# GpSimd adds a head's gates half a head later and makes no low parts in the retrieval

## The reference

```python
def peer(h, w_q, sub_keys, u_tab, v_tab):
    q = (h @ w_q).reshape(B, T, PEER_HEADS, 2, PEER_HALF)
    s = jnp.einsum('bthpd,hpnd->bthpn', q, sub_keys)
    v1, i1 = lax.top_k(s[..., 0, :], K)
    v2, i2 = lax.top_k(s[..., 1, :], K)
    cand = (v1[..., :, None] + v2[..., None, :]).reshape(B, T, PEER_HEADS, K * K)
    cidx = (i1[..., :, None] * PEER_NKEYS + i2[..., None, :]).reshape(B, T, PEER_HEADS, K * K)
    top_s, pos = lax.top_k(cand, K)
    eidx = jnp.take_along_axis(cidx, pos, axis=-1)
    gates = jax.nn.softmax(top_s, axis=-1)
    ...
        u = jnp.take(u_tab, ib, axis=0)
        act = jax.nn.gelu(jnp.einsum('btd,bted->bte', hb, u), approximate=False)
        vv = jnp.take(v_tab, ib, axis=0)
        return jnp.einsum('bte,bted->btd', gb * act, vv)
```

## Time and profile before

| | us |
|---|---|
| median of 3 runs | 1904.72 (1902.17 to 1913.51) |
| profiled execution | 1909.61 |
| its span, first to last instruction | 1906.1 |
| mean granted TensorE clock | 0.963 |
| busy: TensorE | 1756.6 (92%) |
| busy: VectorE | 1314.3 (69%) |
| busy: GpSimd | 866.5 (45%) |
| busy: ScalarE | 716.8 (38%) |

### The profile page before, as it was taken

One profiled execution on the slowest core, in us unless ns is written; L12 is line 12 of the kernel. 1 busy time (PEld: TensorE's weight loads), 2 busy tenths in 40 slices (PEclk: granted clock), 3 DMA queues, 4 the chain that ended last, 5 costly groups with the idle time before them and its releaser, 6 DMA issues. The chain is left out here.

```text
span 1906.1 us, 28988 instructions
## 1 busy us (share of the span) xinstructions
PE 1756.6 (92%) x11226; PEld 1551.3 (81%) x11226; DVE 1314.3 (69%) x2623; ACT 716.8 (38%) x1133; POOL 866.5 (45%) x529
## 2 busy tenths in 40 slices
PE   4999999999989988898798779987999999999998
PEld 2667888888779978897798779986998888888887
DVE  5983444542242566875687779975868888888887
ACT  4442233322253323332332337772333333333334
POOL 2333222244434366676567655533534444444440
PEclk9999899999989989998898889998999999999999
DMA  9663221023214476686687659997979999999994
GB/s 347 232 232 112 101 79 35 24 89 100 88 56 165 158 219 191 197 241 185 182 217 211 201 164 307 332 327 248 361 264 353 376 376 371 372 373 374 374 362 154
DMA packets 187602, 436.05 MB, mean 229 GB/s; under 512 B 34376, under 2 KB 95944, under 8 KB 187360
## 3 DMA queue, kind: packets, MB, share of 16 engines
q1 hardware_dynamic: 113824, 275.29, 41.2%
q0 software_dynamic: 55296, 134.31, 22.3%
q10 hardware_dynamic: 18368, 24.94, 3.6%
HBM read 385.11 MB, written 49.35 MB: 228 GB/s over the span
## 5 line engine op out<-in xcount | busy, mean ns | idle before, releaser
L223 POOL DMA_INDIRECT own_rows<-in_peer_v_dram,own_row x128 | 211.5, 1652 | 266.8 <-DVE y_own L2139 258.1
L2033 PE MATMUL banks<-v_hi,coef_lo 128*128 128x512 f32 x756 | 294.4, 389 | 0.0
L2033 PE MATMUL banks<-v_lo,coef_hi 128*128 128x512 f32 x756 | 294.4, 389 | 0.0
L2033 PE MATMUL banks<-v_hi,coef_hi 128*128 128x512 f32 x756 | 294.1, 389 | 0.1
L246 POOL DMA_INDIRECT gate_scratch<-gates,add_at x128 | 213.4, 1668 | 106.8 <-DVE top_half L1619 51.2
L223 POOL DMA_INDIRECT own_rows<-in_u_rows_dram,own_row x128 | 165.0, 1289 | 190.9 <-DVE own_rows L1777 86.5
L1460 PE MATMUL banks<-h_hi,wring_hi 128*128 128x384 f32 (+2 forms) x560 | 200.7, 358 | 54.6 <-POOL wring_lo L1558 54.2
L1460 PE MATMUL banks<-h_lo,wring_hi 128*128 128x384 f32 (+2 forms) x560 | 199.0, 355 | 0.0
L1460 PE MATMUL banks<-h_hi,wring_lo 128*128 128x384 f32 (+2 forms) x560 | 198.2, 354 | 0.0
L2076 ACT ACTIVATE coef_hi<-coef 128x384 fp32r<-128x384 f32 x128 | 67.1, 525 | 272.8 <-DVE coef L2163 272.8
L1510 ACT ACTIVATE wring_hi<-weight_ring 128x1024 fp32r<-128x1024 f32 x68 | 72.2, 1061 | 252.3 <-PE banks L1460 250.8
(11 more groups left out here) (394 smaller groups left out, 4092.7 us busy)
## 6 DMA issues: line engine op xcount, KB each, us to landing
weight_ring<-in_peer_v_dram SPq DMA_DIRECT2D x128, 512.0 KB, 6.3
weight_ring<-in_peer_u_dram SPq DMA_DIRECT2D x88, 512.0 KB, 4.2
ada<-in_w_ada_dram SPq DMA_DIRECT2D x48, 512.0 KB, 5.9
gate_tiles<-gate_scratch SPq DMA_DIRECT2D x32, 768.0 KB, 7.5
gelu_scratch<-gelu_early ACTq DMA_DIRECT2D x112, 192.0 KB, 4.0
gelu<-gelu_scratch SPq DMA_DIRECT2D x112, 192.0 KB, 6.7
weight_ring<-in_w_merge_dram SPq DMA_DIRECT2D x32, 512.0 KB, 3.4
gate_scratch<-gate_block SPq DMA_DIRECT2D x32, 512.0 KB, 8.0
```

The costliest lines, as they stand in the source:

```text
L223: pool.indirect_dma_start(own_rows[:, n % R], None, tables[n // NS], bass.IndirectOffsetOnAxis(ap=own_row[:, n % NS:n % NS + 1], axis=0)). ...
L2033: last = nc.tensor.matmul(y_bank(t, half)[:], w[:, j, t * P:(t + 1) * P], x[:, j, c], start=(first and n == 0), stop=False)
```

## The change

1. `by_pool` is true only for n < DVE_FROM = 9: VectorE makes the other 27 low parts that GpSimd made, at their places in `fill`.
2. GpSimd's adds move by half a head. At j = 0 to 7 of head h it makes the second eight adds of head h - 2, at j = 8 it waits for the gates of head h - 1, and at j = 8 to 15 it makes the first eight adds of that head. The retrieval has 104 adds instead of 112, the scatter stage 24 instead of 16.
3. DOT_HEADS has 80 row products in the retrieval instead of 64. So U_DONE is 112 instead of 96, the expert stage uses 144 own rows instead of 160, and OWN_GELU is tile 7 instead of 12.

```diff
-DOT_HEADS, DOT_ITER = (0,) + (9,) * 6 + (10,), 8
-POOL_LO = True
+DOT_HEADS, DOT_ITER = (0,) + (11,) * 4 + (12,) * 3, 8
...
-OWN_GELU = 12
+OWN_GELU = 7
...
     if p < EXP_TILES - N_EARLY:
-        return 2 if p == OWN_GELU - 2 else 3
+        return 1 if p == OWN_GELU - 2 else 3
     if i >= 30:
         return int(j < 3)
-    return 2 if p % 11 == 0 else 1
+    return int(p % 18 > 0)
...
         def by_pool(n):
 
-            return n < DVE_FROM or POOL_LO and (n < FIRST[1] + HR and n % 2 == 0 or n % 4 == 2)
+            return n < DVE_FROM
...
-                for n in (*range(HR - 1, DVE_FROM), *pieces_of(0)):
-                    if by_pool(n):
-                        rest(n)
+                for n in range(HR - 1, DVE_FROM):
+                    rest(n)
                 at = 0
+                half = NSC * TOPK // 2
                 for h in range(1, PH):
                     before = sum(DOT_HEADS[:h])
                     pool.wait_ge(*V.after("own_row", h - 1))
-                    todo = pieces_of(h)
                     for j in range(TOPK):
-                        for n in todo[j * len(todo) // TOPK:(j + 1) * len(todo) // TOPK]:
-                            if by_pool(n):
-                                rest(n)
                         while at < before + R + DOT_HEADS[h] * (j + 1) // TOPK:
                             fetch(pool, at)
                             at += 1
-                        if j == 0:
+                        if j == TOPK // 2:
                             pool.wait_ge(*VG.after("gate", h - 1))
-                        for n in range(j * NSC, (j + 1) * NSC):
-                            add_gates(pool, h - 1, n)
+                        for n in range(j * half // 8, (j + 1) * half // 8):
+                            if n < half and h > 1:
+                                add_gates(pool, h - 2, half + n)
+                            elif n >= half:
+                                add_gates(pool, h - 1, n - half)
...
-                for n in range(NSC * TOPK):
-                    g_["add_gates"](pool, PH - 1, n)
-                    for m in range(n * (U_DONE - DOTS) // (NSC * TOPK), (n + 1) * (U_DONE - DOTS) // (NSC * TOPK)):
-                        fetch(pool, DOTS + R + m)
+                adds = [(PH - 2, n) for n in range(NSC * TOPK // 2, NSC * TOPK)] + [(PH - 1, n) for n in range(NSC * TOPK)]
+                for m in range(U_DONE - DOTS):
+                    for h, n in adds[m * len(adds) // (U_DONE - DOTS):(m + 1) * len(adds) // (U_DONE - DOTS)]:
+                        g_["add_gates"](pool, h, n)
+                    fetch(pool, DOTS + R + m)
```

## The result

| | before | after |
|---|---|---|
| median of 4 runs | 1906.06 us (1902.17 to 1913.51) | 1849.23 us (1843.21 to 1852.47) |
| ratio after/before, 95% interval | | 0.9694 (0.9654 to 0.9733) |
| span of the profiled execution | 1906.1 us | 1846.5 us |
| mean granted clock | 0.963 | 0.978 |

The change saves 57 us. The forecast was 1840 us and its range 1822 to 1876.

What follows compares the result with a forecast made beforehand. TensorE bounds the expert stage; in the retrieval it stalls for GpSimd's late low parts. 49.9 + 21.4 + 6 - 1.9 - 10 = 65 us off 1904.7 us gave 1840 us, range 1822 to 1876.

Steps and rivals of the forecast that it cites:

- part 1: Retrieval heads 1 to 5: TensorE's stalls for GpSimd's low parts go, 37.9 us idle and 12 us slow clock.
- Part 2: Retrieval: VectorE takes 27 low parts and 16 row products; it paces heads 6 and 7, which get 21.4 us shorter.
- part 4: Losses: 1.9 us for one more add, and 10 us over seven heads for short stops, bounds 0 and 37 us.
- (b): Retrieval: the stall only moves to a mid-head wait of the same size, giving 1901 us; chance 0.09.
- (c): Retrieval: wide VectorE operations hold each of GpSimd's issues, so it gets slower, 1932 us; chance 0.05.
- Part 3: From own_row of the last head to the next stage: 18.9 us become 11.7 us, counted as 6 us gained.
- the landing of adds: Mid-head in the retrieval: GpSimd waits for its earlier adds to land, at no cost up to about 8 us.
- The extra add in the scatter stage: At the scatter stage's end GpSimd has one add more in its last row of issues, costing 1.9 us.
- The second halves: Denser second halves of heads: VectorE needs 1.2 us more than TensorE, with about 6 us of room, so it fits.
- Rival (a): Retrieval: too dense second halves make VectorE pace all heads, losing 37 us instead of 10, 1867 us; chance 0.13.
- The expert stage: 144 own rows in place of 160 change nothing, as TensorE's run hides them; length kept within 2 us.
- the port rule: Retrieval: each VectorE low part holds a GpSimd issue its full 1.13 us, 58.1 us a head, 1857 us; chance 0.05.

Runs made afterwards that it cites:

- lows_only: The kernel before with only the first part of the change: VectorE makes the 27 low parts, adds and row products stay; 1838.28 us, ratio 0.9636.
- one_low: The kernel before, but GpSimd makes one low part in each of heads 1 to 7, VectorE the other 20 of 27; 1896.73 us, ratio 0.9938.
- tail_adds: The changed kernel with head 6's first eight adds moved from head 7 into the scatter stage, which then has 32; 1839.79 us, ratio 0.9642.
- gap_adds: The changed kernel with the second eight adds of a head issued at j = 0 to 5 instead of 0 to 7; 1839.67 us, ratio 0.9638.
- shift_only: The kernel before with only the second part: adds move by half a head, GpSimd keeps its 27 low parts; 1861.86 us, ratio 0.9762.
- fewer_rows: The changed kernel without the third part: 64 row products in the retrieval, 160 own rows in the expert stage; 1839.18 us, ratio 0.9641.
- rows_only: The kernel before with only the third part: 80 row products in the retrieval, 144 own rows in the expert stage; 1919.28 us, ratio 1.0071.
- combined: The changed kernel with gap_adds, tail_adds, 64 row products placed early with none in head 7, and three scatter-stage fetches moved into the expert stage; 1816.89 us, ratio 0.9531.

## Why the prediction was right, and where not

**The bound and part 1: right.** TensorE paced heads 1 to 5 and needed 282.4 us where 281.8 were forecast, idle time and slow clock both gone. lows_only and one_low show the mechanism. own_row of head 5 came 47.2 us sooner, as forecast, and that of head 7 61.2 us sooner, where about 70 were forecast.

**Part 2, VectorE's load: right in size, and again where it decides.** 254.3 us in heads 1 to 5 against a forecast of 256.5, and 99.1 us in heads 6 and 7 against 97.8. The two halves can be told apart: lows_only, with the 16 low parts and no more products, had 242.6 us there, 11.6 us more than before, where 16 x 1.13 = 18.1 us were added; so 6.5 us went with GpSimd's low parts, where the sum had 5; that this is contention is the prediction's reading, and no run shows it otherwise than by this sum. But the two last heads took 105.2 us and not 97.8: head 6 was TensorE's and VectorE's at once (50.26 and 49.88 us busy), and in head 7 VectorE's 49.2 us came with 5.3 us of waits for own rows. The 10 us put down for part 4 covered these 7.4 us; its size was picked between 0 and 37 us, and that it came so near is luck. By the prediction's own sign, "(b) or (c) holds if VectorE waits for own rows", these waits are a small piece of (b): they stand in one head, while heads 1 to 5 fell as forecast.

**Part 3, the end of the retrieval: wrong.** 6 us were to be gained, none was. The step that failed reads "GpSimd has then to add half a head and to fetch, but its last issue there ended some 10 us before the stage did": it took this distance for room. Two things were wrong with it. In the changed kernel the scatter stage starts 6.0 us after the end of GpSimd's last issue, so only about 5 of the old 10.9 us were room: with the old lag of 8.4 us behind own_row the stretch would have been 14.4 us and not 11.7. And the lag grew to 13.3 us, since own_row comes 61 us sooner and GpSimd's last issue only 56 us. 13.3 + 6.0 = 19.3 us is what was measured. VectorE's part of the step held: from own_row to hot_gate's product were 4.7 us, forecast 3.3 + 1.1. With GpSimd's eight adds out of the way (tail_adds) the stretch is 11.3 us, and the forecast was 11.7.

**Part 4, the landing of adds: wrong.** "So it costs nothing up to about 8 us" failed: the waits were 2.3 to 6.9 us, all below that bound, and cost 9.6 us, as gap_adds shows. The bound looked at the room of one fetch. It left out that a wait adds to all that GpSimd has to do in the head, and the estimate of this load (44.5 + 7 = 51.5 us) had no term for it. In heads 2 to 6 the first add came 6.8 us after the own_row ahead of it; in head 7 it came 13.5 us after (1006.84 against 993.36), and 7.0 us after in gap_adds: head 6 has only 50.3 us, and a landing wait of 6.3 us in it. So GpSimd kept up where TensorE sets 56 us a head and fell behind in the last two, by waits and not by port contention.

**The extra add in the scatter stage: near, in part by luck.** 1.9 us forecast; the stage grew by 2.2 us. shift_only and gap_adds, whose scatter stage has the same 24 adds and starts at the full clock as before, have 179.8 and 179.9 us there against 178.3 us before: the add costs 1.5 us. The changed kernel starts the stage at a clock of 0.51 behind its stop of 10.0 us, and that was in no term. one_low, with 16 adds and such a start, has 180.7 us.

**The second halves: fine until head 7.** TensorE's waits for VectorE's low parts sum to 8.4 us, below the 15 that would have refuted the step, and none is outside head 7. Rival (a), a density of second halves that costs 37 us, did not occur.

**The expert stage: right.** 599.0 before and 598.5 us after, and 598.3 in fewer_rows with 16 own rows more.

**What the sum hid.** The forecast of 65 us and the result of 57 us agree within the range; the 6 us of part 3 are most of what lies between. Yet the prediction took the change for one thing. The first part is worth 69 us; the second adds nothing to it, and the third costs 10 us. The load of VectorE in heads 6 and 7 said half of this beforehand: 97.8 us against TensorE's 91.9 meant that the five products added there, 5.7 us, are paid, while the term "I count nothing" for the rows that leave the expert stage meant that none is earned. The prediction summed the two and did not set them against each other. The other half, the waits for own rows, it did not have.

**Against the port rule.** The prediction weighed a lock by which VectorE's low parts would hold GpSimd's issues for their full length. In lows_only, with 27 low parts more on VectorE, the adds' mean went from 1668 to 1716 ns, and in the changed kernel to 1727 ns; the medians are 1579 and 1576 ns. That is 59 ns x 128 = 8 us in the whole kernel, where the estimate had 7 us for each head. In lows_only the 92 adds that began beside a low part took 1771 ns in the mean and the other 36 took 1576 ns: 0.2 us each and not the low part's 1.2 us. In the changed kernel six adds of over 1.9 us stood beside no such operation, so not all long issues come from this. The Trainium skill's page "SBUF — State Buffer", section "SBUF: two separate sides", has an exclusive lock that is held for a whole instruction, for a VectorE operation with two SBUF inputs only against a GpSimd operation that reads SBUF. For these low parts the trace shows far less than a whole instruction; whether these issues fall under that condition, no run shows.

**Open.** Why an add lands only after some 8 us in mid-retrieval was not tried. The transfer engines are 0.81 to 0.89 busy there, and whether that matters is not known. Nor was it tried to spread VectorE's low parts by time instead of by number.

## What to carry to other kernels

When an engine that works in order both waits for a late semaphore and makes something that the busiest engine needs, ask what stands behind the wait: one operation of 3 us there cost some 8 us of the kernel, and moving the work off that queue was enough; the order mattered far more than the load. The same holds for filler ahead of the operation that is waited for: in rows_only most stalls got longer with one product of 1.1 us more ahead of `weigh`. Work that another stage hides for nothing earns nothing by being moved earlier, and costs its full time, and what waits come with it, in those stretches where its engine already sets the pace, so place such filler by each stretch's spare time and not evenly. And if one engine is to finish a stage much sooner, check every other engine's last issue against the new end: here GpSimd's last issue, 10.9 us ahead of the stage's end before, took back all that was to be gained there.

## What the runs showed of the hardware

- The indirect transfer with an addition lands late: in head 7 of the changed kernel, at a DMA share of 0.81, 8.5 us passed from the start of one issue to the issue that waited for it. In combined's head 6 a wait of 2.92 us ended 6.1 us after the issue (964.95 to 971.04). No row of the kernel before had shown it.
- A block in which GpSimd issues indirect transfers ends late for all engines: in the changed kernel 6.0 us after the last issue's end (1061.6 to 1067.56) at the retrieval's end, and 5.7 us at the scatter stage's (1242.4 to 1248.1). At the retrieval's end it was 5.9 us in lows_only and 5.4 us in fewer_rows. Where GpSimd's last issues set the end of a stage, the wait ahead of them counts most: with the three fetches behind a wait of 15.93 us moved past the stage's end, TensorE's stop fell from 14.66 to 3.01 us.
- The same stop can be followed by either level of the clock. TensorE waits 3.13 us for hot_gate in both the changed kernel and combined. In the changed kernel the clock behind it was 1.00, and it fell only after the stop of 10.02 us; the windows behind the two stops:

```profile
1052.94:1057.50 4.56, 4.56 (x26) 4.28 (x26) 4.22 (x12) 0.19 (x1) 3.65 (x4) 1.00 0.55 129
1067.56:1072.00 4.44, 4.44 (x19) 4.44 (x20) 3.67 (x6) 2.42 (x4) 0.88 (x1) 0.51 0.29 93
```

  In combined the window behind the stop of 3.13 us was

```profile
1039.00:1047.80 8.80, 7.30 (x26) 7.00 (x27) 4.36 (x13) 0.77 (x3) 0.00 (x0) 0.66 0.01 3
```

  0.51 is nearly the lower level, 1.2 GHz, and in combined the clock was at that level for the first 5 us of its window (0.50 from 1038.9 to 1044). TensorE had been busy there without a stop for all of heads 1 to 7, while in the changed kernel it had stopped for 2.3 and for 4.4 us in head 7. Why the clock fell in the one and not in the other was not tried; it may account for part of the 4 us by which combined is above its expectation.
